# A mixture-of-experts stage: two buffers for gathered rows, the slot table read once, gate's rest products moved, and a second engine that issues weight loads

## The reference

```python
p_grp = softmax(hf @ w_rg + b_rg); g_sel = argmax(p_grp)          # 4 groups
le_sel = (hf @ w_re + b_re).reshape(T, 4, 8)[t, g_sel]            # 8 experts in the group
top_p, top_e = top_k(softmax(le_sel), 2)
w_tok = p_g * top_p / sum(top_p)
# each token goes to its two experts of 32:
y_e = (silu(x @ w_gate[e]) * (x @ w_up[e])) @ w_down[e]           # 1024 -> 512 -> 1024
out[t] = sum of w_tok * y_e over the token's two experts
```

## Time and profile before

| | |
|---|---|
| three executions, us | 2383.56, 2383.42, 5639.24; median 2383.56 |
| profiled execution, us | 2383.28, its span 2381.6 |
| mean granted TensorE clock | 0.953 of full speed |
| busy, share of the span | PE 92%, PEld 66%, DVE 50%, ACT 34%, POOL 5% |
| HBM | 381.91 MB read, 14.73 MB written, 167 GB/s over the span |
| chain that ended last | PE 73%, DMA 11%, DVE 8%, ACT 4% |
| loads of expert weights | 96 of 2048 KB each |

### The profile page before, as it was taken

One profiled execution on the slowest core, in us unless ns is written; L12 is line 12 of the kernel. 1 busy time (PEld: TensorE's weight loads), 2 busy tenths in 40 slices (PEclk: granted clock), 3 DMA queues, 4 the chain that ended last, 5 costly groups with the idle time before them and its releaser, 6 DMA issues.

```text
span 2381.6 us, 29998 instructions
## 1 busy us (share of the span) xinstructions
PE 2198.6 (92%) x11728; PEld 1567.2 (66%) x11728; DVE 1197.0 (50%) x1769; ACT 808.8 (34%) x1462; POOL 120.9 (5%) x163
## 2 busy tenths in 40 slices
PE   6999998799999999798993989999999899999997
PEld 3788657533333333366783977888887687888885
DVE  4899575400000000257748346777625564877822
ACT  3222452322223222344552334223324463222421
POOL 0000000111111111100003000000000000000000
PEclk9999999899999999899996799999999899999999
DMA  9442105579999999601110012222223201222221
GB/s 386 170 177 91 73 14 208 205 325 396 398 425 388 403 389 405 267 36 71 71 71 1 2 71 85 92 106 106 79 104 136 71 1 71 106 106 98 79 106 71
DMA packets 35287, 384.60 MB, mean 161 GB/s; under 512 B 8960, under 2 KB 9216, under 8 KB 12288
## 3 DMA queue, kind: packets, MB, share of 16 engines
q1 hardware_dynamic: 27520, 374.95, 39.8%
q0 software_dynamic: 7680, 8.44, 1.0%
HBM read 381.91 MB, written 14.73 MB: 167 GB/s over the span
## 4 chain that ended last, share of the span: by engine, by line
PE 73%; DMA 11%; DVE 8%; ACT 4%; issue 3%; POOLq 0%; SPq 0%; POOL 0%; ACTq 0%; DVEq 0%
PE PS L636 18%; PE PS L638 18%; PE PS L637 18%; DMA A<-h_tokens,idx 7%; PE PS L902 6%; DMA h<-wexp 2%; PE PS L863 2%; PE PS L909 1%; DVE A L1882 1%; PE PS L1032 1%; DMA x<-xt_in 1%; PE PS L853 1%; PE PS L589 1%; ACT A L1475 1%; PE PS L596 1%
## 5 line engine op out<-in xcount | busy, mean ns | idle before, releaser
L637 PE MATMUL PS<-h_r,w_hi_r 128*128 128x512 f32 x1104 | 432.8, 392 | 0.0
L636 PE MATMUL PS<-h_hi_r,w_hi_r 128*128 128x512 f32 x1056 | 424.0, 402 | 8.8 <-DVE A L1882 3.3
L638 PE MATMUL PS<-h_hi_r,ring_r 128*128 128x512 f32 x1056 | 413.4, 391 | 0.0
L2181 DVE TENSOR_TENSOR ring_r<-ring,w_hi_r 128x1024 fp32r<-128x1024 f32 x196 | 238.6, 1222 | 343.2 <-ACT w_hi_r L1485 343.1
L1485 ACT ACTIVATE w_hi_r<-ring 128x1024 fp32r<-128x1024 f32 x196 | 206.2, 1058 | 563.4 <-PE PS L638 327.9
L636 PEld LDWEIGHTS PS<-h_hi_r,w_hi_r 128*128 128x128 f32 x1056 | 199.7, 189 | 63.2 <-issue 10.5
L637 PEld LDWEIGHTS PS<-h_r,w_hi_r 128*128 128x128 f32 x1104 | 209.7, 190 | 47.6 <-issue 4.8
L638 PEld LDWEIGHTS PS<-h_hi_r,ring_r 128*128 128x128 f32 x1056 | 199.7, 189 | 42.3
L2170 DVE TENSOR_TENSOR A<-A,PS 128x512 f32<-128x512 f32 x16 | 11.0, 687 | 383.7 <-PE PS L863 383.7
L863 PE MATMUL PS<-A 128*64 128x512 f32 x768 | 170.8, 601 | 2.0 <-ACT A L1449 2.0
L1882 DVE SCALAR_TENSOR_TENSOR A<-A,vec 128x511 f32<-128x511 f32 (+15 forms) x216 | 160.1, 741 | 6.7
(11 more groups left out here) (469 smaller groups left out, 3485.1 us busy)
## 6 DMA issues: line engine op xcount, KB each, us to landing
A<-wexp SPq DMA_DIRECT2D x64, 2048.0 KB, 12.6
ring<-wall SPq DMA_DIRECT2D x63, 2048.0 KB, 8.1
ring<-wexp SPq DMA_DIRECT2D x16, 2048.0 KB, 19.3
h<-wexp SPq DMA_DIRECT2D x16, 2048.0 KB, 18.6
A<-wada SPq DMA_DIRECT2D x12, 2048.0 KB, 15.3
x<-xt_in SPq DMA_DIRECT2D x2, 2048.0 KB, 11.2
A<-y_assignments SPq DMA_DIRECT2D x4, 1024.0 KB, 7.9
h_tokens<-A SPq DMA_DIRECT2D x4, 512.0 KB, 3.0
```

The source lines that it names most:

```text
L636: mm(out, w[0], x_[0], start=first, stop=False)
L637: mm(out, w[0], x_[1], start=False, stop=False)
L638: return mm(out, w[1], x_[0], start=False, stop=last_)
L2181: tt(ring_r[:, slot, :, cols], ring[:, slot, :, cols], w_hi_r[:, :, cols].bitcast(F32), ALU.subtract).then_inc(S("w_lo"), 1)
```

## The change

- **Rows.** `xg` becomes two sets; the gather of pair i+2 is issued when pair i's rows have been transposed. Both fixed pairs 0 and 1 get their indices from a one-hot (two sets of one-hots, index products and additions ahead of the loop).
- **Table.** The table in HBM is laid out so that two DMAs read it whole into `places` once. In the loop POOL copies a pair's column out of it. The arithmetic of the positions has five more operations on 128 columns.
- **Gate's rest.** The rest products become two groups: gate's right behind gate's main, up's right behind up's main. Each lies on all four quarters: even k on two, odd k on the other two, so that two halves of each sum have to be added: ScalarE copies one half, VectorE adds the other. `m_pc` counts six groups a pair.
- **Loads.** Gates are loaded as soon as the gate's two groups are done, ups when up's are. The downs of every odd pair are issued by ScalarE, behind the even pair's last down product and ahead of its copy of the rest outputs.

```diff
-        xg = [A[:, 40:42, :], A[0:QUARTER, 42:44, :]]
+        xg = [[A[:, 40:42, :], A[0:QUARTER, 42:44, :]], [A[:, 55:57, :], A[0:QUARTER, 57:59, :]]]
         x_main, x_rest = A[:, 44:46, :], A[:, 46, 0:KD * QUARTER]
-        hid_main, hid_rest = A[:, 47, :], A[0:HALF, 48, 0:256]
+        hid_main, hid_rest, up_rest = A[:, 47, :], A[0:HALF, 48, 0:256], A[0:HALF, 48, 256:512]
...
+        def doubles_less_one(eng):
+            return eng.value_load(blki[0:1, 2 * PAIRS_ALL + 1:2 * PAIRS_ALL + 2], min_val=DOUBLES_MIN - 1, max_val=DOUBLES_MAX - 1)
...
-            for j in range(2):
-                sp.wait_ge(S(f"xg{j}"), 16)
+            for q in range(2):
+                sp.wait_ge(S(f"xg{q}"), 32)
             down_of(1, wexp[1:2])
             gate_of(1, 1, wexp[3:4])
-            for j in range(2):
-                sp.wait_ge(S("m_pc"), m_done(0, 2))
-                up_of(j, wexp[2 + j:3 + j])
 
             n = doubles(sp)
+            m = doubles_less_one(sp)
...
             with sp.Fori(1, n) as d:
                 done = 2 * PRODUCTS * d
                 before, first, second = experts(2 * d - 1), experts(2 * d), experts(2 * d + 1)
+                rwait(sp, S("m_pc"), done + m_done(-2, 1))
                 gates(0, first)
-                rwait(sp, S("m_pc"), done + m_done(-2, 4))
-                downs(before)
-                rwait(sp, S("m_pc"), done + m_done(-1, 2))
+                rwait(sp, S("m_pc"), done + m_done(-2, 3))
+                ups(before)
+                rwait(sp, S("m_pc"), done + m_done(-1, 1))
+                gates(1, second)
+                rwait(sp, S("m_pc"), done + m_done(-1, 3))
                 ups(first)
-                gates(1, second)
-                rwait(sp, S("m_pc"), done + m_done(-1, 4))
+                rwait(sp, S("m_pc"), done + m_done(-1, 5))
                 downs(first)
-                rwait(sp, S("m_pc"), done + m_done(0, 2))
-                ups(second)
-            rwait(sp, S("m_y1"), 2 * n)
-            downs(experts(2 * n - 1))
-            rwait(sp, S("m_sg"), 4 * n)
+            last = experts(2 * m + 1)
+            rwait(sp, S("m_pc"), 2 * PRODUCTS * m + m_done(0, 3))
+            ups(last)
+            rwait(sp, S("m_sg"), 8 * n)
+            for q in range(2):
+                rwait(sp, S(f"xg{q}"), 32 * n + 32)
...
-            pe.wait_ge(S("rg"), 4)
-            for t in range(NT):
-                for lo, n, e, bank in ((0, HALF, 0, 5), (HALF, HALF, 1, 5), (P, QUARTER, 0, 4)):
-                    last = mm(PS[lo % P:lo % P + n, bank, 0:2], onehot[:, t, lo:lo + n], C("mine")[:, 4 * t + 2 * e:4 * t + 2 * e + 2], start=t == 0, stop=t == NT - 1)
-            last.then_inc(S("rank"), 1)
+            for f in range(FIXED):
+                pe.wait_ge(S("rg"), 4 + f)
+                for t in range(NT):
+                    for lo, n, e, bank in ((0, HALF, 0, 5), (HALF, HALF, 1, 5), (P, QUARTER, 0, 4)):
+                        v = 4 * (NT * f + t) + 2 * e
+                        last = mm(PS[lo % P:lo % P + n, bank + 2 * f, 0:2], onehot[f][:, t, lo:lo + n], C("mine")[:, v:v + 2], start=t == 0, stop=t == NT - 1)
+                last.then_inc(S("rank"), 1)
...
+            def rest_of(w):
+
+                for k in range(KD):
+                    for half in range(2):
+                        g = HALF * (k % 2) + QUARTER * half
+                        last = mm(PS[g:g + QUARTER, 5, 0:256], x_rest[:, k * QUARTER:(k + 1) * QUARTER], w[0][:, k, 256 * half:256 * (half + 1)],
+                                  start=k < 2, stop=k >= KD - 2)
+                last.then_inc(S("m_pc"), 1)
...
-            rows_T(16)
+            rows_T(0, 32)
             n = doubles(pe)
             with pe.Fori(0, n) as d:
                 for q in range(2):
...
                         pe.wait_ge(S(f"wg{q}{j}"), 16 * d + 16)
                     pe.wait_ge(S("m_x"), 4 * d + (2 * q + 1))
                     main_of(3, moe_gate[q])
+                    pe.wait_ge(S("m_x"), 4 * d + (2 * q + 2))
+                    pe.wait_ge(S("m_y1"), 2 * d + (q + 1))
+                    rest_of(moe_gate[q])
                     for j in range(2):
                         pe.wait_ge(S(f"wu{j}"), 32 * d + 16 * (q + 1))
                     main_of(4, moe_up)
-                    pe.wait_ge(S("m_x"), 4 * d + (2 * q + 2))
-                    pe.wait_ge(S("m_y1"), 2 * d + (q + 1))
-                    for k in range(KD):
-                        for t in range(4):
-                            w = (moe_gate[q], moe_up)[t // 2][0]
-                            last = mm(PS[QUARTER * t:QUARTER * (t + 1), 5, 0:256], x_rest[:, k * QUARTER:(k + 1) * QUARTER],
-                                      w[:, k, 256 * (t % 2):256 * (t % 2 + 1)], start=k == 0, stop=k == KD - 1)
-                    last.then_inc(S("m_pc"), 1)
-                    pe.wait_ge(S("m_h"), 4 * d + (2 * q + 1))
+                    pe.wait_ge(S("m_h"), 8 * d + (4 * q + 1))
+                    rest_of(moe_up)
+                    pe.wait_ge(S("m_h"), 8 * d + (4 * q + 2))
                     for k in range(4):
                         last = nc.tensor.transpose(PS[:, 3, k * P:(k + 1) * P], hid_main[:, k * P:(k + 1) * P], ident)
                     last.then_inc(S("m_tr"), 1)
-                    rows_T(32 * d + 16 * (q + 2))
-                    rwait(pe, S("m_h"), 4 * d + (2 * q + 2))
+                    rows_T(1 - q, 32 * d + 32 * (q + 1))
+                    rwait(pe, S("m_h"), 8 * d + (4 * q + 4))
                     for k in range(2):
...
                     done, turned = 2 * PRODUCTS * d, 8 * d
                     act.wait_ge(S("m_pc"), done + m_done(q, 0))
                     a_(hid_main, PS[:, 3, :], ACT.Silu).then_inc(S("m_sg"), 1)
-                    act.wait_ge(S("m_pc"), done + m_done(q, 2))
-                    a_(hid_rest, PS[0:HALF, 5, 0:256], ACT.Silu).then_inc(S("m_sg"), 1)
+                    act.wait_ge(S("m_pc"), done + m_done(q, 1))
+                    a_(hid_rest, PS[HALF:P, 5, 0:256], ACT.Copy).then_inc(S("m_sg"), 1)
+                    act.wait_ge(S("m_h"), 8 * d + (4 * q + 1))
+                    a_(hid_rest, hid_rest, ACT.Silu).then_inc(S("m_sg"), 1)
+                    act.wait_ge(S("m_pc"), done + m_done(q, 3))
+                    a_(up_rest, PS[HALF:P, 5, 0:256], ACT.Copy).then_inc(S("m_sg"), 1)
                     act.wait_ge(S("m_tr"), turned + (4 * q + 3))
                     a_(hT_main, PS[:, 3, :], ACT.Copy).then_inc(S("m_ht"), 1)
                     rows_out(turned + (4 * q + 4))
-                    act.wait_ge(S("m_pc"), done + m_done(q, 3))
+                    act.wait_ge(S("m_pc"), done + m_done(q, 4))
                     rwait(act, S("sc0"), 32 * d + 16 * (q + NT))
                     a_(yb[0], PS[:, 6:8, :], ACT.Copy).then_inc(S("m_y0"), 1)
-                    act.wait_ge(S("m_pc"), done + m_done(q, 4))
+                    act.wait_ge(S("m_pc"), done + m_done(q, 5))
+                    if q == 0:
+                        for j in range(2):
+                            of = wexp[bass.ds(act.value_load(blki[0:1, bass.ds(4 * d + (2 + j), 1)], min_val=0, max_val=E - 1), 1)]
+                            act.dma_start(moe_dn[j], of[:, 2].rearrange("a p k n -> p (a k) n")).then_inc(S(f"wd{j}"), 16)
...
+            for f in range(FIXED):
+                link(stt(key[f], rank[:, :, 2 * f:2 * f + 2], 1.0, asg[2][:, :, 2 * f:2 * f + 2], ALU.add, ALU.mult))
+                tt(onehot[f][:, :, 0:P].rearrange("p a (e b) -> p a e b", e=2), C("iotar")[:, 0:HALF].rearrange("p (a e b) -> p a e b", a=1, e=1).broadcast_to(X5),
+                   key[f].rearrange("p a (e b) -> p a e b", b=1).broadcast_to(X5), ALU.is_equal)
+                link(tt(onehot[f][:, :, P:PAIR_ROWS], C("iotar")[:, HALF:CAP].rearrange("p (a b) -> p a b", a=1).broadcast_to([P, NT, QUARTER]),
+                        key[f][:, :, 0:1].broadcast_to([P, NT, QUARTER]), ALU.is_equal))
+                nc.vector.memset(er[3], 1.0).then_inc(S("rg"), 1)
...
+            link(tt(er[5], er[5], C("slot2"), ALU.add))
+            for f in range(FIXED):
+                dve.wait_ge(S("rank"), 2 + f)
+                tt(idx[:, f, 0, :], PS[:, 5 + 2 * f, 0:2], C("nobody"), ALU.add).then_inc(S("posi"), 1)
+                tt(idx[0:QUARTER, f, 1, :], PS[0:QUARTER, 4 + 2 * f, 0:2], C("nobody")[0:QUARTER], ALU.add).then_inc(S("posi"), 1)
...
+            over = asg[2]
+            link(tt(over, rank, by_expert(er[6]), ALU.subtract))
+            link(stt(asg[4], over, 0.0, by_expert(er[5]), ALU.is_ge, ALU.mult))
             link(tt(asg[3], asg[3], asg[4], ALU.add))
+            for rows_in in range(PAIR_ROWS, T - HALF, PAIR_ROWS):
+                link(ts(asg[4], over, float(rows_in), float(1 - COLS * PAIR_ROWS), ALU.is_ge, ALU.mult))
+                link(tt(asg[3], asg[3], asg[4], ALU.add))
...
 
             with dve.Fori(0, n) as d:
                 for q in range(2):
```

(65 more changed lines are left out.)

52 lines of the change are left out of this document (18 added, 34 removed).

## The result

Seven executions of the changed kernel have a median of 2364.23 us (2357.84 to 2368.57), seven of the one before 2380.44; the ratio is 0.9928, with a 95% interval of 0.9911 to 0.9946. So it is faster by 0.7%, 16 us: the interval lies clear of 1, but the gain is within the 2% that count as the same. One of the seven runs before, at 5639.24 us, is an outlier that the ratio leaves out. The profiled execution took 2366.6 us, its span 2364.8 against 2381.6. I had forecast 2349 as the likeliest and 2338 to 2371 as the range.

The account below looks back on a forecast made before the run. It took the expert stage as bound by TensorE and DMA locked together, the DMA harder. The stage's end moving from 990.3 to 956 saves 34 us: 2383.3 - 34 = 2349 us, range 2338 to 2371.

Parts of the forecast that it names:

- main case: Expert stage runs at TensorE's pace first, then the DMA's, and ends at 956: 2341 to 2358 us, chance 0.62.
- first rival: DMA is already nearly full by share, since small packets and row-wise gathers may cost more than their bytes: 2366, chance 0.18.
- the rows' wait near 0: Sign in the trace: TensorE's wait for gathered rows in the expert stage, 24.1 us before, nearly vanishes.
- 40 us stretches at 423 to 428 GB/s without holes: Sign in the trace: DMA rate from 485 us on, with no holes of 4 us under 300 GB/s.
- Rows: Two buffers for gathered rows give a 14.4 us gather 30 us of cover; the 24.1 us of waiting go.
- TensorE's pair of 29.0: TensorE's time for an undisturbed pair: 28.74 us, with 0.2 added for the gate's rest split off.
- ScalarE's issues: ScalarE issuing odd pairs' downs takes 2.4 us ahead of its quarter-row copy, with 2.9 us to spare: no cost.
- The head: Work ahead of the expert loop: a second one-hot delays pair 0's indices by 0.5 us, and the stage's start by 0.8.
- T0: Time of TensorE's first expert product: 470.6 + 0.8 = 471.4 us, the delay between 0.4 and 2.5.
- The floor of 30.75 a pair: DMA limit in the expert stage: 13.1 MB a pair at 426 GB/s take 30.75 us, whatever the order of work.
- third rival: Slower: ScalarE's queue takes half the bandwidth, odd pairs' ups come up to 6.5 us late; 66 us lost, 2390, chance 0.08.
- The rule against the change: Skill's limit of about 358 GB/s per core: a pair could not go under 36.6 us, so nothing could be gained.

Follow-up runs that it names:

- e3: The kernel before the change with only the two row buffers, the second one-hot and the table read once added: 2371.63 us, ratio 0.9958.
- e2: e1 with each weight load moving seven of its eight slices, the products as many and as long: 2330.95 us, ratio 0.9794.
- e5: e1 with POOL's early memset moved from 341 us to behind the first transposed tokens, near 450 us: 2360.02 us, ratio 0.9917.
- e4: e1 with half of the main gate and up products left out, all loads as they are: 2354.63 us, ratio 0.9887.
- e1: The changed kernel with SyncE issuing the odd pairs' downs too, so all weight loads stand in one queue: 2359.93 us, ratio 0.9914.

## Why the prediction was right or wrong

It was right in its direction, in its range and in the mechanism, two limits of which the DMA's is the harder. The likeliest value was 15 us too low. The measured 2364 is above the main case's own 2341 to 2358; it lies in the stated range only because that also covers the first rival, whose mechanism did not happen at that size. That much of the hit is luck. The stage was to end at 956 and ends at 975.7. Of its signs, the rows' wait near 0 came true; 40 us stretches at 423 to 428 GB/s without holes did not (372 and 395). By its own steps:

- **Rows.** Right: the wait of 24.1 us is gone. "Late next is a weight load" was right too; e3 shows how much: 27.2 us. (The gather that it puts some 5 us into a pair is issued 3.9 in, 666.56 - 662.71; nothing hangs on it.)
- **TensorE's pair of 29.0.** Right: 28.98 in pair 1, and in all fifteen pairs of e2. The cost of the split rest, 0.2 taken, is 0.24.
- **ScalarE's issues.** Their direct cost was forecast as 2.4 us ahead of the copy, with 2.9 to spare. They are issued 0.9 and 2.1 us after the pair's end and nobody waits for the copy. Right.
- **The head.** T0 from the indices was right: of the 3.5 us by which the products begin later, 1.0 lies between the mixer's last work and them, 0.8 forecast. The other 2.5 us came from ahead of the stage. About 0.9 is there after the first weight loads, 1.4 arises between 370 and 380 us, behind a gap of TensorE of 4 us (it ends at 367.56 in the kernel before), where its clock was lower:

```profile
370.00:380.00 10.00, 10.00 (x45) 8.20 (x44) 3.96 (x6) 1.90 (x3) 0.00 (x0) 0.97 0.03 11
```

```profile
370.00:380.00 10.00, 10.00 (x37) 8.04 (x36) 3.96 (x6) 1.35 (x3) 0.00 (x0) 0.79 0.17 71
```

  The traces of all the variants have 0.69 to 0.83 there, also e5's with the memset moved. What sets it is open, and for the kernel before there is one trace.
- **The floor of 30.75 a pair: the step that was mis-sized.** e4 measures 31.40. The step divided the bytes by the mean rate, which holds if all parts of a load land together. They do not, and TensorE waits for the last: of the 0.65, 0.36 is the drift of the parts, 0.07 the rows' size, 0.22 the rate that rows bring down. 0.65 x 12 pairs is 7.8 us of the 19.7. The first rival's 2366 is the number nearest to what was measured, but of its mechanism ("row-wise gathers may cost the engines more than their bytes") e4 shows 0.2 us a pair, 2 to 3 us, where its number is 17 above the main case's.
- **The two queues.** The third rival's effect happened: ups of odd pairs late by up to 7.6 us (6.5 forecast), the clock down behind it (9.69 against 7.02), and, against my expectation, the DMA without work afterwards. I had argued that a backlog would be there. It is not, because the load that TensorE waits for is at that moment the last in its queue. The loss is 7.2 us in the profiles, 4.4 in the medians, not the 66 of the rival, since the DMA's floor absorbs the rest. The rival's reason, half the bandwidth for all of the load, is not what the steps show: the first parts were on time and the last one late. The rule of the Trainium skill ("DMA: Bandwidth & Descriptors", the section on queues, rings and completion order), that an engine goes round-robin between its queues packet by packet, agrees in that both queues move at once. The shares of 84 to 13 do not contradict it, since most of the ups had landed; why the last part was 6.6 us later than in one queue it does not say.
- **The rule against the change** (the Trainium skill, same page, the section on bandwidth), about 358 GB/s, does not bind here: e4 holds 423 GB/s over 377 us. The same section gives it as each core's part when both cores of the HBM domain stream, which no run here shows, and for one core alone 425 GB/s at 16 MB, with which the trace agrees. The prediction took the rule without that condition.

The sum nearly closes: 956 + 2.7 (T0) + 7.8 (floor) + 7.2 (second queue) = 973.7, against 975.7; 2.0 are left over. The 7.2 is the difference between two profiles, so what this tests is the rest: 966.5 for e1, whose stage ends at 968.54. The floor is e4's; e1's own pace from 572.28 to 887.26 is 31.50. After the stage the two profiles differ by 2.2 us (2364.8 - 975.7 against 2381.6 - 990.3), which nothing in the change explains and which I take for spread (not shown). One kernel beats both: the changed one without ScalarE's loads, 2359.93, ratio 0.9914 to the one before.

## What to carry to other kernels

When a wait is removed in a stage that two limits share, work out the pace of each alone and forecast the slower; then test them alone, by fewer bytes and by fewer products, as the two numbers (28.98 and 31.40 here) say at once what is left to gain. A second DMA queue added no bandwidth here, where the engines were full (408 GB/s against 415 with one); it only changed the order, and the load that TensorE waited for had its last part later. A load can be used only when its last part is in: bytes over the mean rate give a floor that is too low when the parts of loads drift apart, as they did here once the DMA had no holes. Count the loads that a window of the profile holds against those that were used in it: 72.9 against 72 was half of the floor's error here.

## What was not expected of the hardware

- The parts of one load land over a span that grows while the DMA has no holes: 3.4 us at the ups of pair 2 and 9.7 at those of pair 14 in e4, at most 3.7 in the kernel before, which has holes. After a hole the changed kernel's loads are together again (1.5 us for the ups issued at 592.41).
- With ScalarE's queue filled 11 us after the ups of pair 3 were issued in SyncE's, the first parts of those ups land about as in one queue (16.1 us after issue against 15.6), the last 6.6 us later (26.7 against 20.1).
- The queue of row-wise gathers and scatters takes the engines at 350 to 370 GB/s (1.14 MB in 3.2 us, 1.81 in 4.9) where the weight loads beside them move 426 (38.18 MB in 89.7 us). Its 4 KB packets alone move 409; most of the rest is packets of 4 bytes.
- TensorE's clock after one and the same gap came back later in all eight traces of the changed kernel and its variants (0.69 to 0.83 in 370 to 380 us) than in the one of before (0.97), for 1.4 us in the changed one; in e5 POOL, which had the memset, runs nothing from 300 to 380 us.
